# Attention pairs: scaling, turns and values one step later each, probabilities in two buffers, first output products between the last turns

## The reference, cut to what matters

```python
def masked_softmax(s, mask):
    s = jnp.where(mask, s, NEG)
    m = jnp.max(s, axis=-1, keepdims=True)
    e = jnp.exp(s - m) * mask
    return e / jnp.maximum(jnp.sum(e, axis=-1, keepdims=True), 1e-30)
...
    s = jnp.einsum('btgrd,bsgd->bgrts', qg, kwc).astype(jnp.float32) * scale + head_bias(dist_w)
    p = masked_softmax(s, mask_w[None, None, None])
    o_win = jnp.einsum('bgrts,bsgd->btgrd', p.astype(vwc.dtype), vwc)
    o = gc[..., 0:1] * o_cmp + gc[..., 1:2] * o_slc + gc[..., 2:3] * o_win
...
    mixed = jnp.concatenate([rms_norm(o_attn, attn_out_norm[layer]),
                             rms_norm(o_conv, conv_out_norm[layer])], axis=-1)
    x = x + mixed @ w_out[layer]
```

## Time and profile before

| what | value |
|---|---|
| time, median of 3 | 2343.96 us (2339.43 to 2344.37) |
| time of the profiled execution | 2343.87 us |
| its span, first to last instruction | 2342.0 us |
| mean granted clock of TensorE | 0.964 |
| busy in the span | PE 94%, DVE 18%, ACT 12%, POOL 3% |
| attention loop of layer 0 | 130.75 to 307.53 us |
| attention loop of layer 1 | 959.93 to 1134.14 us |
| output products of a layer | 56 us |
| feed-forward of layer 0 | 379 to 836 us |
| experts of layer 1 | 1262 to 2305 us |

### The profile page before, as it was taken

The page is one execution under the profiler, slowest core; times in us unless marked ns, Lnnn a source line. Parts: engine busy times, 40 slices in busy tenths (PEclk is TensorE's granted clock), DMA queues, the critical chain, the costliest instruction groups (busy, mean ns, idle before and its releaser), DMA issues.

```text
span 2342.0 us, 30066 instructions
## 1 busy us (share of the span) xinstructions
PE 2207.9 (94%) x12858; PEld 1616.3 (69%) x12858; DVE 432.5 (18%) x1236; ACT 270.4 (12%) x736; POOL 69.7 (3%) x77
## 2 busy tenths in 40 slices
PE   7999998999999989999975999999999999999994
PEld 3544444444444445444455999999999999999994
DVE  2146622000000021356322001010010101010102
ACT  1223311000000012233100000000000000000000
POOL 1100000000000011000000000000000000000001
PEclk9999998999999989999976999999999999999997
DMA  8100006222210402010008556767777787878743
GB/s 327 45 37 37 31 10 251 90 72 72 74 70 0 199 9 72 36 37 1 1 37 350 225 213 237 287 251 287 267 285 273 276 300 278 313 282 306 292 182 117
DMA packets 43924, 382.32 MB, mean 163 GB/s; under 512 B 5362, under 2 KB 5394, under 8 KB 14480
## 3 DMA queue, kind: packets, MB, share of 16 engines
q1 hardware_dynamic: 36208, 355.68, 40.5%
q0 software_dynamic: 4704, 14.40, 1.9%
q10 hardware_dynamic: 2880, 10.32, 1.1%
HBM read 367.94 MB, written 14.54 MB: 163 GB/s over the span
## 4 chain that ended last, share of the span: by engine, by line
PE 90%; DVE 5%; issue 2%; DMA 1%; ACT 1%; POOL 1%; POOLq 0%; DVEq 0%; ACTq 0%
PE ps L382 29%; PE ps L391 14%; PE ps L1019 13%; PE ps L1028 6%; PE ps L855 6%; PE ps L795 6%; PE ps L1001 5%; PE ps L906 2%; PE ps L918 2%; PE ps L893 1%; PE ps L801 1%; PE ps L868 1%; DVE work L1076 1%; DVE work L1204 1%; PE ps L363 1%
## 5 line engine op out<-in xcount | busy, mean ns | idle before, releaser
L382 PE MATMUL ps<-work,arena 128*128 128x136 f32 (+3 forms) x5632 | 704.9, 284 | 0.7 <-issue 0.7
L382 PEld LDWEIGHTS ps<-work,arena 128*128 128x128 f32 x5632 | 687.0, 191 | 1.2 <-issue 0.8
L391 PE MATMUL ps<-hid,arena 128*128 128x136 f32 (+3 forms) x2816 | 364.7, 283 | 0.0
L391 PEld LDWEIGHTS ps<-hid,arena 128*128 128x128 f32 x2816 | 348.4, 191 | 0.1
L1019 PE MATMUL ps<-hT,arena 128*128 128x512 f32 x704 | 304.7, 596 | 0.8 <-issue 0.8
L1019 PEld LDWEIGHTS ps<-hT,arena 128*128 128x128 f32 x704 | 134.6, 191 | 170.5 <-issue 170.5
L552 DVE TENSOR_TENSOR hid<-sg,ps 128x136 f32<-128x136 f32 (+3 forms) x176 | 52.7, 299 | 900.4 <-ACT sg L653 899.8
L855 PE MATMUL ps<-hT,arena 128*128 128x512 f32 x384 | 203.6, 629 | 8.6 <-DVE zc L1130 5.3
L653 ACT ACTIVATE sg<-ps 128x136 f32<-128x136 f32 (+3 forms) x176 | 50.6, 287 | 928.4 <-PE ps L382 928.4
L1028 PE MATMUL ps<-arena 128*128 128x512 f32 x352 | 151.3, 592 | 0.8 <-DVE arena L1301 0.8
L795 PE MATMUL ps<-arena,hT 128*128 128x512 f32 (+1 forms) x384 | 131.0, 500 | 0.0
(11 more groups left out here) (204 smaller groups left out, 1031.2 us busy)
## 6 DMA issues: line engine op xcount, KB each, us to landing
arena<-m_w SPq DMA_DIRECT2D x176, 1536.0 KB, 6.5
arena<-f_gu SPq DMA_DIRECT2D x22, 1024.0 KB, 5.0
arena<-w_cv SPq DMA_DIRECT2D x8, 1536.0 KB, 21.6
arena<-f_dn SPq DMA_DIRECT2D x11, 1024.0 KB, 4.8
arena<-w_o SPq DMA_DIRECT2D x4, 2048.0 KB, 7.5
arena<-w_q SPq DMA_DIRECT2D x2, 2048.0 KB, 11.5
arena<-w_kv SPq DMA_DIRECT2D x2, 2048.0 KB, 15.9
arena<-bias_by_query_and_key SPq DMA_DIRECT2D x2, 2048.0 KB, 8.8
```

The lines of the kernel that those rows point to most:

```text
L382: m = mm(ps[:, s % 2, j * CAP:j * CAP + W], w[:, k, :], xT[:, k, 0:W], start=(k == 0), stop=(k == KD - 1))
L391: m = mm(ps[:, 2 + j // 2, (j % 2) * CAP:(j % 2) * CAP + W], down_w[s % NSLOT][:, j * P:(j + 1) * P], hid[:, s % 2, 0:W], start=(s == 0 an ...
```

## The change

All of pair p's later work moves by one step: the scaling from DVE's step p to p+1, the turns from PE's step p+1 to p+2, their copies likewise, the values from p+2 to p+3. The even turn now stands ahead of the scores in PE's step, the odd one behind the first fill, and the values behind the second; on DVE the copy stands first in the step, ahead of the scores. The probabilities have two buffers of a pair each, the second in a free part of the arena (1024 columns). What ends a tile of queries moves by one or two steps too. The loop has one more step. In the steps 32, 33 and 34 PE does three half products of the first output tile (j = 0 whole, j = 1 its first half), and the sums of squares stand behind j = 2 instead of j = 1.

```diff
-        sb_s, sb_p = w2[:, 0], w2[:, 1]
+        sb_s = w2[:, 0]
+        sb_p = [w2[:, 1], arena[:, A_PROB:A_END].rearrange("p (b n) -> p b n", b=2)]
...
+                def out_products(t, j, ks):
+                    part, hf = j // 2, j % 2
+                    m = None
+                    for k in ks:
+                        m = mm(ps[:, 4 * (t % 2) + j, :], mixT[:, 4 * part + k, t * P:(t + 1) * P],
+                               WO[part][:, k, hf * 512:(hf + 1) * 512], start=(k == 0), stop=(k == 3))
+                    return m
+
-                for p in range(NP + 2):
+                for p in range(NP + 3):
                     t, q = p // 8, p % 8
                     f = STEP_FILL[p] if p < len(STEP_FILL) else (0, 0, 0)
+                    if 2 <= p < NP + 2:
+                        turn(2 * p - 4)
                     if p < NP:
                         scores(p)
                     fill(f[0])
-                    if 1 <= p <= NP:
-                        turn(2 * p - 2)
+                    if p == NP:
+                        pe.wait_ge(wo_in[0], 16 * (L + 1))
+                        pe.wait_ge(sb_done, NU * (L + 1))
+                        pe.wait_ge(mix_done, TT * L + 1)
+                    if p >= NP:
+                        out_products(0, (p - NP) // 2, (0, 1) if p != NP + 1 else (2, 3))
+                    if 2 <= p < NP + 2:
+                        turn(2 * p - 3)
                     fill(f[1])
-                    if p >= 2:
-                        values(p - 2)
-                    if q == 0 and t:
+                    if p >= 3:
+                        values(p - 3)
+                    if q == 1 and t:
                         cmp_values(t - 1)
-                    if 1 <= p <= NP:
-                        turn(2 * p - 1)
                     fill(f[2])
                     if p == 3:
                         cmp_keys()
-                    if q == 3 and t:
+                    if q == 5 and t:
                         o_total(t - 1)
...
-                    for j in range(4):
-                        part, hf = j // 2, j % 2
-                        for k in range(4):
-                            m = mm(...)
-                        if t == 0 and j == 1:
+                        m = out_products(t, j, (2, 3) if t == 0 and j == 1 else range(4) if t or j else ())
+                        if t == 0 and j == 2:
                             o_total(TT - 1)
                             conv_totals()
...
-                for p in range(NP + 2):
+                for p in range(NP + 3):
                     t, q = p // 8, p % 8
+                    if 2 <= p < NP + 2:
+                        pt_copy(2 * p - 4)
                     if p < NP:
                         scores(2 * p)
                         scores(2 * p + 1)
                     if 1 <= p <= NP:
-                        pt_copy(2 * p - 2)
-                    if p < NP:
-                        scale(p)
+                        scale(p - 1)
...
-                    if q == 1 and t:
+                    if q == 2 and t:
                         evacuate(t - 1)
-                    if q == 2 and t:
+                    if q == 3 and t:
                         o_reduce(t - 1)
...
-                    if u >= 2:
-                        se.wait_ge(pt_ps, NU * L + u - 1)
+                    if u >= 4:
+                        se.wait_ge(pt_ps, NU * L + u - 3)
...
-                    if 1 <= p <= NP:
-                        pt_copy(2 * p - 1)
+                    if 2 <= p < NP + 2:
+                        pt_copy(2 * p - 3)
...
-                    if q == 1 and t:
+                    if q == 2 and t:
                         o_squares(t - 1)
```

More of the change, by code:

```diff
@@ L80 @@
 A_Z = A_MIX + KD * S
-A_END = A_Z + 2 * G * ZC
+A_PROB = A_Z + 2 * G * ZC
+A_END = A_PROB + 2 * S
 ARENA = NSLOT * SLOT
@@ L145, in build @@
         junk = work[:, 2 * D:3 * D]
-        k_tmp, sqb = sb_s[:, 0, 0:256], sb_p[:, 0, :]
+        k_tmp, sqb = sb_s[:, 0, 0:256], sb_p[0][:, 0, :]
         yc, sqsum = arena[:, A_KC:A_KC + S], arena[:, A_KC + S:A_KC + 2 * S]
@@ L172, in build @@
         mixT = arena[:, A_MIX:A_Z].rearrange("p (k n) -> p k n", k=KD)
-        Z = arena[:, A_Z:A_END].rearrange("p (a g n) -> p a g n", a=2, g=G)
+        Z = arena[:, A_Z:A_PROB].rearrange("p (a g n) -> p a g n", a=2, g=G)
         T = arena[:, A_T:A_T + H * S].rearrange("p (h n) -> p h n", h=H)
@@ L905, in turn @@
                     for i in range(t + 1):
-                        m = tr(ps[:, 2, i * P:(i + 1) * P], sb_p[:, u % 2, i * P:(i + 1) * P], ident)
+                        m = tr(ps[:, 2, i * P:(i + 1) * P], sb_p[u // 2 % 2][:, u % 2, i * P:(i + 1) * P], ident)
                     m.then_inc(pt_ps, 1)
@@ L994, in layer @@
                         pe.wait_ge(mix_done, TT * (L + 1))
-                    b0 = 4 * (t % 2)
                     if t >= 2:
@@ L998, in layer @@
                     for j in range(4):
-                        part, hf = j // 2, j % 2
-                        for k in range(4):
-                            m = mm(ps[:, b0 + j, :], mixT[:, 4 * part + k, t * P:(t + 1) * P],
-                                   WO[part][:, k, hf * 512:(hf + 1) * 512], start=(k == 0), stop=(k == 3))
-                        if t == 0 and j == 1:
+                        m = out_products(t, j, (2, 3) if t == 0 and j == 1 else range(4) if t or j else ())
+                        if t == 0 and j == 2:
                             o_total(TT - 1)
@@ L1203, in scale @@
                     for g in range(G):
-                        v.tensor_scalar(sb_p[:, g, 0:n], sb_p[:, g, 0:n], d[:, g:g + 1], gts[:, t, R * g + r, 1 + b:2 + b],
+                        v.tensor_scalar(sb_p[p % 2][:, g, 0:n], sb_p[p % 2][:, g, 0:n], d[:, g:g + 1], gts[:, t, R * g + r, 1 + b:2 + b],
                                         ALU.mult, ALU.mult).then_inc(scaled, 1)
@@ L1403, in probs @@
                     se.wait_ge(sb_done, NU * L + u + 1)
-                    if u >= 2:
-                        se.wait_ge(pt_ps, NU * L + u - 1)
+                    if u >= 4:
+                        se.wait_ge(pt_ps, NU * L + u - 3)
                     if u == 0:
                         se.wait_ge(red_done, 9 * L + 8)
-                    act(sb_p[:, u % 2, 0:n], sb_s[:, u % 2, 0:n], ACT.Exp, bias=negm[:, u % 16:u % 16 + 1], scale=-1.0,
+                    act(sb_p[u // 2 % 2][:, u % 2, 0:n], sb_s[:, u % 2, 0:n], ACT.Exp, bias=negm[:, u % 16:u % 16 + 1], scale=-1.0,
                         accum_out=den[:, u % 16:u % 16 + 1]).then_inc(p_done, 1)
```

1 line of the change is left out of this document (removed).

## The result

The changed kernel takes 2314.64 us (median of 4, 2313.77 to 2315.58) against 2343.74 us before: a ratio of 0.9879, 95% interval 0.9863 to 0.9895, 29.1 us less. The forecast was 2312 us, with a range from 2303 to 2328. The profiled execution took 2315.58 us.

A forecast was written before the change was run, and what follows sets the result against it. PE's work bounds the attention loops, with 49 us lost to a ring of waits; 16 us would stay, 33 less, minus 1 us for the clock: 2343.9 - 32 = 2312 us. Range for 8 in 10: 2303 to 2328 us.

The forecast's parts named there:

- What bounds the kernel: Attention loops: PE's work alone some 151 us; waits in a ring through three engines lose 49 us together.
- Ring and place of the loss: Inside each step: DVE's 61.3 us of waiting at the reciprocal for ACT's exponential go, except in the first step.
- Head: Steps 0 to 3: about 12.2 us of PE's work, 1.3 us left over; before, 5 us over the work.
- Body: Steps 4 to 29: waits of 3.7 us stay where DVE's work stands ahead of the copy; before, about 10.6 lost.
- Tail: Steps 30 to 34: steps 30 and 31 take 4.2 us each; left over 2.4 us, before 10.4 (layer 1 8.0).
- Left over: Each layer's loop: 1.3 + 3.7 + 2.4 = 7.4 us lost, 8 with unseen waits; together 16 against 49 before.
- The sums of squares: Before tile 1: one product of 3.44 us between instead of two, 1.4 us of cover left, costed at nothing.
- The clock: Both loops: mean clock 0.98 or more; at 1.0 they would save at most 10.6 us, within the 49.
- rival 1: Loops: waits for the scaling vanish, those for copies (8.9 of layer 0's 16.5 us) stay; 2328 us, chance 0.16.
- 3: Loops: bound by PE's work, the waits only move to other lines, within 4 us of 2344; chance 0.04.
- Rival 2: Tail and head of the loops: the clock still falls, some 7 of 10.6 us stay lost; 2319 us, chance 0.14.
- Rival 4: Head of DVE's step: late copy makes odd turns wait; slower from 0.8 us lost in each step; chance 0.03.

The follow-up runs named there:

- buffers_only: Kernel before with the second probability buffer alone (exponential waits for turn u-4 instead of u-2), no step moved: 2313.95 us, ratio 0.9878.
- delay_copy: Changed kernel with an unused 0.68 us DVE addition between the wait for the even turn and its copy, steps 4 to 31: 2329.32 us, ratio 0.9944.
- shift_only: Changed kernel with all output products together behind the loop again, no half products between the last turns: 2321.21 us, ratio 0.991.
- buffers_products: Kernel before with the second buffer and the three half products in its steps 32 and 33, nothing shifted: 2308.49 us, ratio 0.9855.
- cmp_early: Changed kernel with the third tile's compressed scores, scaling and turn one step earlier (steps 19, 20, 21): 2312.71 us, ratio 0.9871.
- one_buffer: Changed kernel with one probability buffer, ACT's copy and small work ahead of the exponentials: 2329.52 us, ratio 0.9938.
- delay_end: Changed kernel with an unused 0.68 us DVE addition behind the scaling, steps 4 to 31: 2318.98 us, ratio 0.9891.
- tail_fills: Changed kernel with the last eight fills over steps 27 to 31 as 2, 2, 2, 1, 1 instead of 2, 3, 3, 0, 0: 2314.29 us, ratio 0.9876.

## Why the prediction was right, and where it was not

**What bounds the kernel**: right. The ring of buffer, exponential and scaling was the loss, and PE's work, put at 151 us a loop, is the floor. The best loop came to 160.83 - 5.16 = 155.7 us; PE was busy in it for 152.6 us, so the floor was set 1 to 2 us too low for that order, and lower still for the changed one (below).

**Ring and place of the loss**: right in what goes, wrong in what does it. The prediction took shift and buffer for one thing ("In the new order the scaling of p-1 stands in step p", and only then that the exponential needs turn u-4). Its step "DVE's 61.3 us of waiting go" came true, but buffers_only shows that 50 of them had their cause in ACT's wait for turns, not in the place of the scaling. The wait that was called one ring was two waits in a row, and taking the first away leaves 11.3 us of the second. Nowhere did the prediction ask what each half is worth alone.

**Head**: steps 0 to 3 took 13.2 us from scores to scores, forecast 12.2 + 1.3 = 13.5. That this is so near is partly luck: PE waited 0.35 us there, not 1.1, and its work took 12.9 us, not 12.2.

**Body**: its waits were right, mostly to the tenth. PE's waits in layer 0 were 0.33 us (step 9), 0.35 (12), 0.17 (18), 0.81 (19), 1.24 (21) and 0.16 (27), 3.1 together; forecast 0.3, 0.4, 0.2, 0.8, 1.3 and 0.5, and 0.2 in step 6, where there was none. They were all waits for DVE's copy behind small work that starts at the end of PE's step. delay_copy confirmed the slack of most other steps.

**Tail**: the loop was mis-sized. Steps 30 and 31 took 4.59 us each, not 4.2. Timeline of step 31:

```profile
282.04 0.63 PE L908 MATMUL ps<-cst,arena 128*128 128x128 f32 x4 [0.92 <-ACT work L1427]
...
282.71 0.69 DVE L1223 COPY arena<-ps 128x512 f32<-128x512 f32 x1 [1.11 <-PE ps L908]
...
283.76 0.69 DVE L1203 CUSTOM_DVE_ANT_0 work<-ps,arena 128x512 f32<-128x512 f32 x1 [0.36 <-PE ps L895]
...
284.50 0.72 ACT L1419 ACTIVATE arena<-work,st 128x512 f32<-128x512 f32 x1 [1.19 <-DVE st L1203]
...
285.22 0.71 ACT L1419 ACTIVATE arena<-work,st 128x512 f32<-128x512 f32 x1
...
285.92 0.56 ACT L1427 COPY arena<-ps 128x512 f32<-128x512 f32 x1
286.63 0.63 PE L908 MATMUL ps<-cst,work 128*128 128x128 f32 x4 [1.29 <-ACT arena L1427]
```

My sum had turn, DVE's copy, two scores, one exponential, ACT's copy. The path of these rows is turn, PE's scores, one score on DVE, two exponentials (0.72 + 0.71), ACT's copy. DVE's copy ends 0.36 us before PE's scores are there, since these now stand behind the turn, and so is off the path; delay_copy bears this out: 0.68 us more ahead of the copy made the step only 0.14 us longer. From the turn of step 30 to the end it took 20.5 us. I had 2 x 4.2 us, 6.1 us of work in the steps 32 to 34 (the figure in my expectation of shift_only) and 5.16 us of moved products, 19.7.

**Left over**: forecast 8 us a layer over PE's 151; measured 9.8 and 11.4. Layer 1's loop, 162.4 us, lies outside the 157 to 161 us of the prediction. Of the difference 0.8 us is the tail, and 1.6 in layer 1 the clock. The rest, 9.8 - 8 - 0.8 = 1.0 us, stands there although head and body's waits came out 0.3 and 0.6 us better than forecast and 0.6 us had been put down for the unseen: some 2.5 us a layer were missing in the sum. The prediction's term for this was "each engine's busy time stays". The row that answers to it is PE's busy time, for the new order itself needs more of PE. At full clock and with the same work (926 and 925 records) PE is busy for 160.25 us in the changed kernel's first loop and for 158.07 in that of buffers_products. A small part can be read in the timelines: a turn between a fill and scores takes 0.53 us to the next start at width 512 (258.91 to 259.44 in the changed kernel), one between values and a fill 0.49 (268.93 to 269.42 in buffers_products). I haven't tried a kernel for this, so why the order costs 2.2 us is open.

**The sums of squares**: right, covered. POOL's power ends at 306.3, the last product of tile 0 at 307.9:

```profile
303.34 1.03 PE L958 MATMUL ps<-cst,arena 128*128 128x1 f32 x8
...
304.66 1.65 POOL L1508 TENSOR_TENSOR st<-st,cst 128x8 f32<-128x8 f32 x1 [168.62 <-DVE st L1066]
```

**The clock**: 1.00 and 0.99, forecast 0.98 or more. It did not fall in the steps 30 and 31, where I had looked for it, but in step 21 of layer 1, behind a wait of 1.24 us. The Trainium skill ("TensorE: Matmul & The Clock Gate", "A second HAM failure mode: psum-queue depth-cycling") says that frequent short idles between groups of products make the clock go up and down. The tail of shift_only agrees: waits of 0.92, 1.28 and 0.88 us, granted clock 0.58. In cmp_early the wait went, and no record was slow in either layer; that the wait was the cause is likely by this, not shown, since with the wait in place the clock also stayed up in 3 of 10 loops (last section).

**The rivals**: rival 1 (half the waits stay) is out, as is 3. Rival 2 (the clock falls in the tail and the head) didn't come there; the clock cost 1.6 us in step 21 of layer 1 instead. Rival 4, the wait at the head of DVE's step, had a mechanism that exists and a size that was wrong: the waits of the body and delay_copy's two-fill steps show it. All that the shift costs against the unshifted order with two buffers is 6 to 7 us, of which the waits are 1.6, far from the 0.8 us in each of 64 steps, some 50 us, from which the change would be slower.

## What to carry to other kernels

Where engines wait for one another in a ring, ask for each buffer and each moved step by itself what it frees: here a second buffer, with the change of one wait, gave all of the gain, and the deeper pipeline around it cost 6 to 7 us. In a hand-written order, walk through the steps with the durations of the trace and write down for each wait when its value is wanted and when it comes; that found all six waits of the body here, and one that didn't come. Put work that ends late behind the copy that another engine waits for, not ahead of it, and spread the filler products until no step is without (1.9 us a loop here). Before you explain a difference of 1 or 2 us between two traces, set them side by side step by step and read the granted clock: here one step at half clock was as large as the effect of several of the edits.

## What the runs showed of the hardware

I had not expected that a single wait of 1.24 us could cost more by the clock than by itself: in layer 1 it was followed by some 3.3 us at 1.2 GHz, 1.6 us lost, in layer 0 of the same execution by nothing.

It is not the neighbouring work that decides. Five kernels (the changed one, shift_only, one_buffer, delay_end and tail_fills) have this wait of 1.24 or 1.25 us in step 21, ten loops in all. In seven of them step 21 took 7.24 to 7.47 us with a granted clock of 0.72 over some 6 us, in three 5.83 us at full clock: layer 0 of the changed kernel and of shift_only, layer 1 of one_buffer. The changed kernel, shift_only and tail_fills do the same work in the same order up to this step. Nor does the length of the wait decide: in delay_copy it was 1.84 us in both layers, with no slow record behind it and a granted clock of 1.00 over both loops.

```profile
232.05 0.52 PE L909 MATMUL ps<-cst,arena 128*128 128x128 f32 x3 [1.84 <-DVE arena L1226]
232.41 1.02 PE L858 MATMUL ps<-hT,arena 128*128 128x512 f32 x2
```

So the price of a short wait is not fixed: 1.2 us if the clock holds, 2.7 to 2.9 if it doesn't. What decides between the two is open.
